# Norm weights put on the latents in the projection, GpSimd's subtraction moved behind its eliminations, one tile of key rows per gate tile, the first chunk's keys loaded alone

## What is computed

```python
hproj = rmsnorm(x, ln_in_w) @ w_in
qkv, z_g, b_g, a_g, cq, ckv, kr, z_m = split(hproj)          # 3072, 1024, 8, 8, 512, 512, 64, 1024 columns
qkv, new_conv = causal_short_conv(qkv, conv_buf, w_conv)      # then silu; q and k are l2-normed
o_g, new_ssm = gated_delta_rule(q, k, v, g, beta, ssm0)       # blocks of positions, inverse of a unit triangular matrix
qm = rmsnorm(cq, q_norm_w) @ w_q_up
c_kv = rmsnorm(ckv, kv_norm_w)                                # also an output: new_latent (the "key rows")
o_m = latent_attention(qm, c_kv, ...)
y = rmsnorm(x + concat(o_g * silu(z_g), o_m * silu(z_m)) @ w_out, ln_final_w)
```

## Time and profile before

| | |
|---|---|
| median of 3 runs | 2346.05 us (2342.02 to 2347.33) |
| the profiled execution | 2348.15 us, its span 2346.3 us |
| busy share of the span | TensorE 94%, VectorE 45%, ScalarE 30%, GpSimd 10% |
| mean granted TensorE clock | 0.976 of full speed |
| TensorE busy, 100 to 1100 us / 1100 to 1300 us (projection) | 988.5 of 1000 / 179.8 of 200 |
| TensorE busy, 1300 to 1500 us (mostly recurrence) | 161.55 of 200 |

### The profile page before, as it was taken

The page is one execution under the profiler, slowest core; times in us unless marked ns, Lnnn a source line. Parts: engine busy times, 40 slices in busy tenths (PEclk is TensorE's granted clock), DMA queues, the critical chain, the costliest instruction groups (busy, mean ns, idle before and its releaser), DMA issues. The chain is left out here.

```text
span 2346.3 us, 34713 instructions
## 1 busy us (share of the span) xinstructions
PE 2203.9 (94%) x14309; PEld 2146.4 (91%) x14309; DVE 1052.9 (45%) x1736; ACT 695.0 (30%) x1140; POOL 244.5 (10%) x269
## 2 busy tenths in 40 slices
PE   6999999999999999998997988699999999999997
PEld 5999999999999999988997978598898889999996
DVE  4354444523234441122361666455445464545553
ACT  4322222212121122222111444333334233344433
POOL 1000000000001000100400277100000040000000
PEclk9999999999999999999998999799999999999998
DMA  5122212222223333334545575521111128576563
GB/s 158 56 78 71 79 57 83 63 73 64 71 91 99 110 108 91 109 100 130 96 92 128 148 192 130 142 68 32 58 51 47 47 75 240 150 231 180 163 187 113
DMA packets 401953, 249.94 MB, mean 107 GB/s; under 512 B 78185, under 2 KB 379930, under 8 KB 401698
## 3 DMA queue, kind: packets, MB, share of 16 engines
q1 hardware_dynamic: 388834, 207.70, 33.5%
q10 hardware_dynamic: 10800, 32.75, 3.6%
q0 software_dynamic: 2192, 7.69, 1.1%
HBM read 185.99 MB, written 57.78 MB: 104 GB/s over the span
## 5 line engine op out<-in xcount | busy, mean ns | idle before, releaser
L941 PE MATMUL proj_acc<-h_hn_hi,proj_w_hi 128*128 128x352 f32 x2256 | 743.1, 329 | 0.0
L941 PE MATMUL proj_acc<-h_hn_hi,proj_w_lo 128*128 128x352 f32 x2256 | 724.6, 321 | 0.0
L941 PE MATMUL proj_acc<-h_hn_lo,proj_w_hi 128*128 128x352 f32 x2256 | 724.3, 321 | 0.0
L941 PEld LDWEIGHTS proj_acc<-h_hn_lo,proj_w_hi 128*128 128x128 f32 x2256 | 425.8, 189 | 4.9 <-issue 3.9
L941 PEld LDWEIGHTS proj_acc<-h_hn_hi,proj_w_hi 128*128 128x128 f32 x2256 | 424.8, 188 | 5.5 <-issue 4.4
L941 PEld LDWEIGHTS proj_acc<-h_hn_hi,proj_w_lo 128*128 128x128 f32 x2256 | 423.9, 188 | 0.0
L517 DVE TENSOR_TENSOR proj_w_lo<-proj_w_raw,proj_w_hi 128x2048 fp32r<-128x2048 f32 (+1 forms) x49 | 111.3, 2271 | 164.0 <-ACT proj_w_hi L373 163.3
L487 ACT ACTIVATE proj_conv<-proj_acc 128x352 f32<-128x352 f32 x72 | 33.4, 464 | 433.1 <-PE proj_acc L941 433.0
L2044 PE MATMUL mla_big<-all_late,mla_w_hi 128*128 128x352 f32 (+1 forms) x544 | 132.3, 328 | 10.7 <-DVE mla_w_lo L1904 10.2
L2463 PE MATMUL mixo_acc<-all_late 128*128 128x352 f32 x768 | 130.8, 326 | 3.4 <-PEq L1526 3.4
L734 DVE TENSOR_SCALAR proj_conv<-proj_conv,all_cols 128x1059 f32<-128x1059 f32 x24 | 18.5, 772 | 245.6 <-ACT proj_conv L475 245.6
(11 more groups left out here) (328 smaller groups left out, 3511.6 us busy)
## 6 DMA issues: line engine op xcount, KB each, us to landing
proj_w_raw<-in_w_in SPq DMA_DIRECT2D x47, 1024.0 KB, 5.7
mixo_w_raw<-in_w_out SPq DMA_DIRECT2D x47, 1024.0 KB, 6.0
scratch_qkv<-proj_conv ACTq DMA_DIRECT2D x24, 529.5 KB, 2.8
rec_qkv<-scratch_qkv SPq DMA_DIRECT2D x8, 1536.0 KB, 8.1
scratch_gate<-proj_conv ACTq DMA_DIRECT2D x16, 528.0 KB, 2.7
proj_conv<-scratch_qkv SPq DMA_DIRECT2D x32, 256.0 KB, 3.1
proj_conv<-in_x_prompt SPq DMA_DIRECT2D x28, 256.0 KB, 2.9
mixo_xb<-in_x_prompt SPq DMA_DIRECT2D x48, 128.0 KB, 2.2
```

The source lines that it names most:

```text
L941: last = pe.matmul(acc[b][c][0:n, 0:NW], w[:, b, k, 0:n], h[:, k, cut], start=(k == 0 and x == 0), stop=(k == KT - 1 and x == 2))
```

## The change

- `square_sums` ends with one more VectorE instruction per latent tile, which multiplies the evacuated tile by its 128 norm weights. ScalarE stores a latent tile one tile later, in `beside`, after a wait for that instruction. The multiplications by the weights in `latent_rows` (L642) and in `weigh_piece` (L1195) go.
- `latent_rows` on SyncE is split into `load_rows_of` and `store_rows_of`; each gate tile with `latent_of` 15 to 23 stores one tile of key rows and loads the next. The waits of the inversion, its temporary buffer (`tmp`, now in `unit`) and the broadcast factors (`root_all`, now in `ones`) move accordingly; a semaphore `lat_out` of their own counts these stores.
- In GpSimd's loop of `recur` the eliminations come ahead of `low_piece` and `load_piece`.
- At the start of `recur` the keys of the first chunk are loaded alone and first; then SyncE waits for three half clearings (`blank`), loads the blocks, and then queries and values. TensorE turns the first keys without waiting for `set_up`.

```diff
-    ROWS_AT = {LATENT_ROOT + 1 + n: [x for x in (2 * n, 2 * n + 1) if x < TOKEN_TILES] for n in range((TOKEN_TILES + 1) // 2)}
+    LATENT_STEPS = PIECE_STEPS * len(PIECES) + 1
+    rows_of = lambda t: latent_of(t) - LATENT_ROOT - 2
-        rstd_rows, root_all = turned_piece[:, 0:SUB], turned_piece[:, P:2 * P]
+        rstd_rows, root_all = turned_piece[:, 0:SUB], ones[:]
-        tmp = part[:].rearrange("p f t -> p (f t)")
+        tmp = unit[:, 0:2 * BATCH].rearrange("p k n -> p (k n)")
...
@@ project, SyncE
-            def latent_rows(x):
+            def load_rows_of(x):
                 at, n = P * x, TOKENS[x]
                 if x == 0:
-                    sp.wait_ge(tails_stored, 16 * NSUB)
-                else:
-                    sp.wait_ge(lat_step, rows_step(x - 1, PIECE_STEPS))
+                    sp.wait_ge(lat_out, 16 * NSUB)
                 sp.dma_start(row_in[:, :, 0:n], d["latent"]...)
                 sp.dma_start(root_all[:, 0:n], d["rstd"]...)
-                sp.wait_ge(lat_step, rows_step(x, PIECE_STEPS))
+            def store_rows_of(x):
+                n = TOKENS[x]
+                sp.wait_ge(lat_step, rows_step(x, ROW_STEPS))
                 for g in range(NSUB):
                     sp.dma_start(to...[g], row_out[cut, :, 0:n]...)
...
             def beside(t):
                 k = unit_of(t)
-                for x in ROWS_AT.get(latent_of(t), ()):
-                    latent_rows(x)
+                if 0 <= rows_of(t) < TOKEN_TILES:
+                    store_rows_of(rows_of(t))
+                if 0 <= rows_of(t) + 1 < TOKEN_TILES:
+                    load_rows_of(rows_of(t) + 1)
                 if k == -1:
                     operands(0)
...
@@ project, ScalarE
+                f = latent_of(t) - 1
+                if 0 <= f < LATENTS:
+                    act.wait_ge(lat_step, lat_summed(f))
+                    act.dma_start(d["latent"][f], act_out[:, 1 - t % 2, 0:T]).then_inc(stored[1 - t % 2], 16)
...
-                    act.dma_start(d[kind][row], act_out[:, b, 0:T]).then_inc(stored[b], 16)
+                    if kind == "gate":
+                        act.dma_start(d["gate"][row], act_out[:, b, 0:T]).then_inc(stored[b], 16)
...
@@ project, VectorE
                     dve.tensor_reduce(b[:, ...], turned_piece[:, 0:n]..., AX.X, ALU.add).then_inc(lat_step, 1)
+                dve.wait_ge(stored[(LOOPED + f) % 2], stores("latent", f // 2, f % 2))
+                gain = (R_QN, R_KVN)[f % 2] + f // 2
+                dve.tensor_scalar(y[:, 0:T], y[:, 0:T], cols[:, 0, gain:gain + 1], None, ALU.mult).then_inc(lat_step, 1)
...
-                dve.tensor_tensor(raw, raw, cols[:, 0, R_KVN:R_KVN + C_TILES]..., ALU.mult).then_inc(lat_step, 1)
-                dve.wait_ge(lat_step, rows_step(x, 2))
...
-                    dve.wait_ge(tails_stored, rows_stored(PROMPT_TILES))
+                    dve.wait_ge(lt_out, 16 * (UNITS + 1))
+                    dve.wait_ge(at_out, 16 * (UNITS + 1))
...
@@ recur, SyncE
-            inputs(0)
-            sp.wait_ge(set_up, READY)
-            blocks(0)
+            for w in (1, 0, 2):
+                own = slice(HEADS * w, HEADS * w + HEADS)
+                sp.dma_start(qkv[:, 0, own], qkv_d[:, own, 0:P]).then_inc(keys_in if w == 1 else qkv_in[0], 16)
+                if w == 1:
+                    sp.wait_ge(blank, 3)
+                    blocks(0)
             scores(0)
             inputs(1)
+            sp.wait_ge(set_up, READY)
             blocks(1)
...
@@ recur, GpSimd
+            pool.memset(Bo[:, 0], 0.0).then_inc(blank, 1)
+            pool.memset(Bo[:, 1], 0.0).then_inc(set_up, 1)
             pool.dma_start(piece[:, 0:C_TILES], ...)
             pool.dma_start(piece[:, C_TILES], ...)
-            pool.memset(Bo[:], 0.0).then_inc(set_up, 1)
...
-                pool.wait_ge(weighed, half_weighed(x))
-                pool.tensor_tensor(raw, raw, cols[:, 0, NORM[w]:NORM[w] + C_TILES]..., ALU.mult).then_inc(weighed, 1)
...
+                for m in range(LEAVES_TO[c], LEAVES_TO[c + 1]) if c < LEAF_SLOTS else ():
+                    eliminate(m)
                 if done is not None:
                     low_piece(done)
                 if done is not None and done + 1 < len(PIECES):
                     load_piece(done + 1)
-                for m in range(LEAVES_TO[c], LEAVES_TO[c + 1]) if c < LEAF_SLOTS else ():
-                    eliminate(m)
                 if c in piece_at:
                     weigh_piece(piece_at[c])
...
@@ recur, VectorE
-            dve.memset(Xd[:], 0.0).then_inc(set_up, 1)
-            dve.memset(Yd[:], 0.0).then_inc(set_up, 1)
+            for u, sem in ((0, blank), (1, set_up)):
+                dve.memset(Xd[:, u], 0.0).then_inc(sem, 1)
+                dve.memset(Yd[:, u], 0.0).then_inc(sem, 1)
             dve.wait_ge(set_up, READY)
+            dve.wait_ge(blank, 3)
...
@@ recur, TensorE
-            pe.wait_ge(set_up, READY)
...
-                pe.wait_ge(qkv_in[c % 2], 16 * (c // 2) + 16)
+                pe.wait_ge(*((qkv_in[c % 2], queries_in(c)) if c else (keys_in, 16)))
...
             def turn_values(c):
+                if c == 0:
+                    pe.wait_ge(qkv_in[0], queries_in(0))
+                    pe.wait_ge(set_up, READY)
```

More of the change, by code:

```diff
@@ L181, in project @@
         stored = [s.sem(f"stored{u}") for u in range(2)]
-        rows_in, params_T, params_in, half_in, mean_in, rstd_in, diag_ready, quarter_T, weighted, high_in, low_in = (
-            s.sem(n) for n in ("rows_in", "params_T", "params_in", "half_in", "mean_in", "rstd_in", "diag_ready", "quarter_T", "weighted", "high_in", "low_in"))
+        rows_in, params_T, params_in, mean_in, rstd_in, diag_ready, quarter_T, weighted, high_in, low_in = (
+            s.sem(n) for n in ("rows_in", "params_T", "params_in", "mean_in", "rstd_in", "diag_ready", "quarter_T", "weighted", "high_in", "low_in"))
         x_in, squared = [s.sem(f"x_in{n}") for n in range(2)], s.sem("squared")
@@ L197, in project @@
             s.sem(n) for n in ("gm_ready", "exps", "decayed", "qk_in", "scored", "scaled", "masked", "lt_out", "at_out"))
-        lat_step, lat_mean = s.sem("lat_step"), s.sem("lat_mean")
-        lat_summed = lambda f: PIECE_STEPS * len(PIECES) * (f + 1)
+        lat_step, lat_mean, lat_out = (s.sem(n) for n in ("lat_step", "lat_mean", "lat_out"))
+        lat_summed = lambda f: LATENT_STEPS * (f + 1)
         diag_in, step, y_turned, inv_out, rooted = (s.sem(n) for n in ("diag_in", "step", "y_turned", "inv_out", "rooted"))
@@ L357, in _ @@
             beside(TILES - 1)
-            sp.wait_ge(tails_stored, 32 + rows_stored(PROMPT_TILES))
+            sp.wait_ge(tails_stored, 32)
+            sp.wait_ge(lat_out, rows_stored(PROMPT_TILES))
             sp.wait_ge(lt_out, 16 * (UNITS + 1))
@@ L707, in beside @@
                     scale_sample()
-                for x in ROWS_AT.get(latent_of(t), ()):
-                    latent_rows(x)
+                if 0 <= rows_of(t) < TOKEN_TILES:
+                    latent_rows(rows_of(t))
                 if 1 <= latent_of(t) <= LATENTS:
@@ L757, in _ @@
             pool.sem_inc(tail_out, 2)
[L758 to L759 removed]
+            pool.memset(mhalf[:], -0.5).then_inc(padded, 1)
+            pool.wait_ge(padded, 1)
             for t, n in enumerate(TOKENS):
@@ L1060, in recur @@
         piece_in, weighed, piece_hi = (s.sem(n) for n in ("piece_in", "weighed", "piece_hi"))
-        half_weighed, all_weighed, piece_lo = (lambda x, n=n: 3 * x + n + 1 for n in range(3))
+        all_weighed, piece_lo = (lambda x, n=n: 2 * x + n + 1 for n in range(2))
         LEAF_DONE = 2 * SUB + 1
+        blank, keys_in = s.sem("blank"), s.sem("keys_in")
         rso, V_s, kd_s, stat, mix_s, rms_s = (s.sem(n) for n in ("rso", "V_s", "kd_s", "stat", "mix_s", "rms_s"))
@@ L1193, in weigh_piece @@
                 pool.tensor_tensor(raw, raw, piece[:, C_TILES][:, None, :].to_broadcast(full), ALU.mult).then_inc(weighed, 1)
-                pool.wait_ge(weighed, half_weighed(x))
-                pool.tensor_tensor(raw, raw, cols[:, 0, NORM[w]:NORM[w] + C_TILES][:, :, None].to_broadcast(full), ALU.mult).then_inc(weighed, 1)
             def low_piece(x):
```

22 lines of the change are left out of this document (10 added, 12 removed).

## The result

The changed kernel takes 2306.57 us (median of four runs, 2306.40 to 2308.29) against 2346.69 us for the kernel before (median of four runs here): a ratio of 0.9832, with a 95% interval of 0.9815 to 0.985. The gain is 40.1 us; 38 were forecast. The profiled execution took 2306.44 us, its span 2304.6 us, 41.7 less than the span before.

The account below looks back on a forecast made before the run. TensorE works through almost the whole span, so its standstills were the target. Gains of 24 + 16 + 1.5 - 3.5 = 38 us took the profiled 2348.15 us to 2310, 2308 off the median; range 2299 to 2317.

Parts of the forecast that it names:

- The key rows, 24 us: Gate tiles: with one tile of key rows each, TensorE's score products no longer wait for operands; 24 us gained, bounds 12 and 26.
- half the operand waits stay: Rival, gate tiles: row load and 128-byte stores ahead on the queue slow the operands' landing; 12 us less, 2320; chance 0.09.
- The weights on the latents, zero: Latent tiles: eight new VectorE multiplications of 0.77 us each and the later store cost zero, covered by over 10 us.
- GpSimd's loop, 16.0: Recurrence chunks: 20.4 us lost, less charges of 1.5, 2.4 and 0.5; 16.0 us gained, bounds 6 and 20.
- a calmer part of the chunk: Recurrence: the next piece's load now meets less traffic, so 2.4 us was charged for its exposed landing.
- GpSimd becomes the bound: Rival, recurrence: pieces land in 7.3 us, GpSimd's chunk is 23.95 us; gain 27, time 2319; chance 0.17.
- The end, -3.5: End of the recurrence: GpSimd's longer sixth loop ends the sample's inversion copy late; all behind comes 3.5 us later, bounds 2 and 5.
- The start, 1.5: Recurrence's start: blocks issued earlier, queries and values behind them; 1.5 us gained, bounds -1 and 3.
- up to 2.4 us: Recurrence's start: blocks issued at 1270.9 instead of 1273.26 bring TensorE's first triangular product forward by up to 2.4 us.
- The slower rival: Recurrence: GpSimd keeps the port across instructions, L1338 waits 10.2 us instead of 2.9; +14 us, 2360; chance 0.04.

## Why the prediction was right, point by point

- *The key rows, 24 us:* measured 24.3, by the waits that were named, and the operands' cover held even with the multiplication put back. Right in size and place. One sentence of that part was too short: the wait of 4.67 us did cost more than its length (7.5), and the granted clock fell with it; waits of 0.9 to 2.2 us left it at 1.00 and cost about their length (1.2 to 2.5). The rival "half the operand waits stay" is out.
- *The weights on the latents, zero:* their cost is zero, as TensorE's empty view of waits shows. ScalarE's evacuations of a latent tile now come together at its end, behind the waiting store, as foreseen:

```profile
770.12 0.33 ACTq L455 DMA_DIRECT2D scratch_latent<-proj_conv  x1
770.57 1.18 ACT L498 ACTIVATE proj_conv<-proj_acc 128x352 f32<-128x352 f32 x3 [21.96 <-DVE proj_conv L648]
```

  But zero was wrong as its worth. I had counted what this part removes (the multiplication of the rows on VectorE, L1195 on GpSimd) only inside other terms. By itself it would have gained 17 of the 24 us, and without it the reorder on GpSimd would have gained over 13 less. A sum of parts gives each a price; here two parts shared one gain (one brings all of it alone, the other 17 of the 24 us), and another gain needed two parts for most of its size.
- *GpSimd's loop, 16.0:* measured 18.4. The mechanism was right (L1358 short in five chunks, waits for the subtraction gone, GpSimd waiting for its piece, L1349 up to 0.66 us in the chunks); the charges were too large. In sum the five chunks are 105.19 - 103.2 = 2.0 us over the nominal length, where 4.4 were charged: L1358 takes 0.18 to 0.38 us, little over its 0.15, and the piece lands in a median of 4.7 us, the lower bound, not in 5.4. The runs with the subtraction in four instructions show that the reorder also spares TensorE waits for blocks; "a calmer part of the chunk" was right, and worth more than I said.
- *"GpSimd becomes the bound":* half of this rival came true. GpSimd's loop does set the length of four chunks, at 20.9 to 21.3 us and not at 23.95; 2.53 us more in it are paid in full in the mean.
- *The end, -3.5:* measured -2.7, in a stretch that varies by 2 us between kernels with the same code there (see the last section), so only the order in time bears it out. The copy ended 10.2 us into its chunk (10.7 forecast), the power began 4.1 us later than before (4.5 forecast), L1358 was held as before. That the copy would hold L1351 was not in the forecast; it cost little, since the power stands behind the copy on GpSimd anyway.
- *The start, 1.5:* measured -0.2, within its bounds, but the step failed. The gain was there (the first chunk starts 2.5 us nearer to the projection's end) and was given back in the next chunk. Queries and values now go behind the first blocks, so the second chunk's blocks come behind 1 MB more, beside the 1.5 MB of that chunk's own q, k and v; I had followed the queue only to the first triangular product. The step that failed is thus "up to 2.4 us": it took the first triangular product for the end of the path, where a wait of 2.44 us for the next blocks followed. TensorE's later waits were the thing to look at.
- *The slower rival* (GpSimd keeps the port from one instruction to the next) is out: 0.67 us with four instructions in a row.

The errors of +0.3, +2.4, +0.8 and -1.7 us leave +1.8: 39.8 us from the parts, where the medians differ by 40.1. That it came so near is partly luck: the chunks' error and the start's offset each other, and the profiles of before and after also differ by 2.7 us in `project_out`, which no part of the forecast holds.

## What to carry to other kernels

A tiny VectorE instruction with its operands in SBUF can wait for the whole of a long GpSimd instruction (2.90 us instead of 0.15 here): move the long one away or cut it into pieces, and look where its loads land afterwards, since small blocks that landed in 1.9 us took 3.3 to 4.0 where the load came earlier. Price an edit with the other edits present and absent, because parts of one change can share a gain or depend on each other. When a load is moved in a queue, follow the queue past the first user, to the next that waits on it.

## What had not been expected

- The clock: TensorE's standstills of 4.67 us in a gate tile went with a granted clock of 0.90 for that tile, those of 1.5 and 2.2 us with 1.00. Shortening a wait by 3.1 us gained 5.9 us in the first tile (33.12 to 27.26). The length of a wait does not settle it: in the recurrence of the kernel before, five chunks each held one wait of 2.75 to 2.79 us for L1304, and the clock was 1.00 in one and 0.87 to 0.93 in four. Two of them (columns as above), and one of the changed kernel:

```profile
1357.30:1380.70 23.40, 19.35 (x171) 18.69 (x169) 15.99 (x32) 11.33 (x31) 15.81 (x14) 1.00 0.68 170
1380.70:1406.27 25.57, 21.95 (x171) 21.13 (x169) 16.19 (x32) 11.33 (x31) 20.17 (x20) 0.87 0.81 208
```

```profile
1330.36:1351.69 21.33, 19.35 (x170) 18.69 (x169) 13.92 (x32) 11.46 (x31) 14.79 (x16) 1.00 0.80 212
```

  Against 20.69 us, the shortest of the five chunks of the changed kernel, the same wait cost 2.7 us in the first and 4.9 in the second. In the changed kernel all five chunks stand at 1.00. So part of the chunks' 18.4 us is the clock: TensorE's busy time in the five fell from 104.1 to 96.7 us, for the same products.
- `project_out` is the same code in all these kernels and takes 391.6 to 395.1 us. Two of its tiles together take 15.92 us in one execution and 16.12 in another, and sometimes change from the one to the other midway, at a granted clock of 1.00 both times. Each kernel left one profile, so whether this goes with the execution or with the kernel is not shown. The profile after had 15.92 where the one before had 16.12; that is the 2.7 us of the table, which the change doesn't explain. What sets it stays open. It limits what a median can say here to some 3 us, so the verdicts on smaller terms above rest on rows.
- The end of the recurrence varies too. In four kernels whose code there is that of the changed one, which took 52.61 us, it took 52.86, 53.15, 54.05 and 54.84 us, at granted clocks of 0.75, 0.74, 0.70 and 0.70 (0.75 in the changed kernel). So some 2 us of a difference in this stretch can belong to no edit.
